# Delta rule: the values' convolution moved from VectorE to GpSimd, in a two-block kernel on one Trainium2 core

## What is computed

```python
def causal_depthwise_conv_2(x, w):        # width 4, one weight per channel and tap
    return lax.conv_general_dilated(x, w[:, None, :], window_strides=(1,),
        padding=[(CONV_WIDTH - 1, 0)], dimension_numbers=("NWC", "WIO", "NWC"), feature_group_count=c)

qkv_b = jax.nn.silu(causal_depthwise_conv_2(qkv_b, conv_w[i]))
q_b, k_b, v_b = jnp.split(qkv_b, 3, axis=-1)
qb = l2_norm(to_heads(q_b, N_HEADS_GDN))
kb = l2_norm(to_heads(k_b, N_HEADS_GDN))
vb = to_heads(v_b, N_HEADS_GDN)
...
o_b = gated_delta_rule(qb, kb, vb, g, beta)     # in chunks of 64 in the reference
```

## Time and profile before

| | us |
|---|---|
| median of 3 runs | 914.2 |
| lowest and highest | 913.17, 914.21 |
| the profiled execution: its own time | 914.48 |
| its span, from the first to the last instruction | 912.7 |
| PE busy in that span | 883.4 (97%) |
| DVE busy | 595.2 (65%) |
| ACT busy | 519.0 (57%) |
| POOL busy | 24.5 (3%) |

### The profile page before, as it was taken

How to read it: one execution, slowest core, us unless ns; L and a number is a source line. 1 busy time by engine, 2 the same in 40 slices (tenths; PEclk the granted TensorE clock), 3 DMA queues, 4 the chain that set the end, 5 groups by cost and what they waited for, 6 DMA issues and landing times. The chain is left out here.

```text
span 912.7 us, 17954 instructions
## 1 busy us (share of the span) xinstructions
PE 883.4 (97%) x7098; PEld 817.2 (90%) x7098; DVE 595.2 (65%) x971; ACT 519.0 (57%) x910; POOL 24.5 (3%) x36
## 2 busy tenths in 40 slices
PE   8999999999999999998989989899999999999998
PEld 6988899999998999998988979899988999999986
DVE  4689755555556666678685868666758554554576
ACT  6478754444446755657557374845459444444463
POOL 4100300000000000000000000000000000000000
PEclk8999999999999999999999999999999999999999
DMA  9813765555553454544223141415555555556541
GB/s 283 270 51 135 165 199 192 191 192 193 189 184 125 153 180 144 184 140 137 93 71 116 48 139 48 139 49 185 186 196 187 183 186 190 178 193 198 176 168 46
DMA packets 107655, 143.31 MB, mean 157 GB/s; under 512 B 3016, under 2 KB 95432, under 8 KB 107600
## 3 DMA queue, kind: packets, MB, share of 16 engines
q1 hardware_dynamic: 105648, 137.60, 46.6%
q0 software_dynamic: 1744, 4.74, 2.4%
q10 hardware_dynamic: 208, 0.20, 0.1%
HBM read 141.47 MB, written 1.05 MB: 156 GB/s over the span
## 5 line engine op out<-in xcount | busy, mean ns | idle before, releaser
L1180 DVE TENSOR_TENSOR wl<-w_raw,wh 128x1024 fp32r<-128x1024 f32 x251 | 305.3, 1224 | 228.3 <-ACT wh L634 227.7
L1794 PE MATMUL ps<-xTh,wh 128*128 128x256 f32 (+1 forms) x1160 | 331.9, 286 | 0.9 <-DVE xTl L1206 0.8
L1795 PE MATMUL ps<-xTl,wh 128*128 128x256 f32 (+1 forms) x1160 | 326.3, 281 | 0.0
L1796 PE MATMUL ps<-xTh,wl 128*128 128x256 f32 (+1 forms) x1160 | 326.3, 281 | 0.0
L634 ACT ACTIVATE wh<-w_raw 128x1024 fp32r<-128x1024 f32 x251 | 263.3, 1054 | 84.3 <-PE ps L1802 63.1
L1794 PEld LDWEIGHTS ps<-xTh,wh 128*128 128x128 f32 x1160 | 219.4, 189 | 5.0 <-issue 3.3
L1795 PEld LDWEIGHTS ps<-xTl,wh 128*128 128x128 f32 x1160 | 218.3, 188 | 2.1 <-issue 1.2
L1796 PEld LDWEIGHTS ps<-xTh,wl 128*128 128x128 f32 x1160 | 219.3, 189 | 0.0
L1800 PE MATMUL ps<-wh,y 128*128 128x512 f32 x224 | 87.9, 392 | 0.0
L1802 PE MATMUL ps<-wh,y 128*128 128x512 f32 x224 | 87.6, 391 | 0.0
L1801 PE MATMUL ps<-wl,y 128*128 128x512 f32 x224 | 87.1, 389 | 0.0
(11 more groups left out here) (380 smaller groups left out, 1274.1 us busy)
## 6 DMA issues: line engine op xcount, KB each, us to landing
w_raw<-in_w_in_dram SPq DMA_DIRECT2D x42, 1024.0 KB, 5.2
w_raw<-in_w_ff_dram SPq DMA_DIRECT2D x32, 1024.0 KB, 5.3
w_raw<-in_w_ffn_gate_dram SPq DMA_DIRECT2D x11, 1024.0 KB, 5.2
w_raw<-in_w_ffn_up_dram SPq DMA_DIRECT2D x11, 1024.0 KB, 5.3
w_raw<-in_w_ffn_down_dram SPq DMA_DIRECT2D x11, 1024.0 KB, 4.9
w_raw<-in_w_out_dram SPq DMA_DIRECT2D x8, 1024.0 KB, 5.0
w_raw<-in_w_proj_a_dram SPq DMA_DIRECT2D x4, 1024.0 KB, 5.1
w_raw<-in_w_proj_b_dram SPq DMA_DIRECT2D x4, 1024.0 KB, 5.2
```

Of the source, the lines that this page charges most:

```text
L1180: TT(low_part, raw_unit(SLOT[p], j, layout), high_part.bitcast(F32), ALU.subtract).then_inc(w_lo, 1)
L1794: mm(out, wh_, xh, start=first, stop=False)
L1795: mm(out, wh_, xl, start=False, stop=False)
L1796: return mm(out, wl_, xh, start=False, stop=last)
```

## The change

The values' convolution leaves DVE's list (stage 4 of the last attention round, stage 21 of the first three rounds of the delta rule) and becomes a loop of its own on GpSimd, four times. GpSimd waits until unit 5 of the pair has been copied out of PSUM, and from the second pair on until ACT has read the values of the pair before. It then scales by tap 0 into `cvn`, and for each further tap scales into a new buffer `vtap` (two scalings), waits for itself, adds `vtap` to `cvn` (two additions), and waits for itself again before the next tap. It reads the weights in `cw_all` directly. ACT waits on GpSimd's semaphore `cv_val` where it waited on DVE's `cv_out`, and `cv_out` counts two steps a pair instead of three. To make room for the semaphores, four of the first block are merged into others (each wait is for the same event as before). The new buffer takes 512 elements per partition, by which the region `R` grows from 16128 to 16578.

```diff
-REGION = 16128
+REGION = 16578
@@
+        vtap = carve(c4, 2, S)
@@ GpSimd
+            def value_conv(fu, stride, a, b):
+
+                for n in range(2):
+                    pool.wait_ge(emptied[n], along(AFTER[n], fu + 5, stride, a))
+                if b:
+                    pool.wait_ge(silu_v, b)
+                taps = cw_all.rearrange("p t (k h) -> p t k h", k=3)[:, :, 2, :]
+                for j in range(2):
+                    ins = pool.tensor_scalar(cvn[:, 4 + j, :], raw[:, 4 + j, 0:S], taps[:, 0, 2 * b + j:2 * b + j + 1], None, ALU.mult)
+                for tap in range(1, 4):
+                    for j in range(2):
+                        ins = pool.tensor_scalar(vtap[:, j, :], raw[:, 4 + j, tap:tap + S], taps[:, tap, 2 * b + j:2 * b + j + 1], None, ALU.mult)
+                    ins.then_inc(cv_tap, 1)
+                    pool.wait_ge(cv_tap, 5 * b + 2 * tap - 1)
+                    for j in range(2):
+                        ins = pool.tensor_tensor(cvn[:, 4 + j, :], cvn[:, 4 + j, :], vtap[:, j, :], ALU.add)
+                    if tap < 3:
+                        ins.then_inc(cv_tap, 1)
+                        pool.wait_ge(cv_tap, 5 * b + 2 * tap)
+                ins.then_inc(cv_val, 1)
+
+            pool.wait_ge(small2, 16 * 8)
+            pool.wait_ge(filled, 7)
+            value_conv(2 * P_MOBA + 32, 8, 0, 0)
+            for b in range(1, PAIRS):
+                value_conv(2 * P_GDN + 8, 8, b - 1, b)
+
             pool.wait_ge(mg_lo, 4)
@@ ScalarE, gdn_unit
-                        act.wait_ge(cv_out, (pair - 1) * 3 + (c // 2 + 1))
+                        if c < 4:
+                            act.wait_ge(cv_out, (pair - 1) * 2 + (c // 2 + 1))
+                        else:
+                            act.wait_ge(cv_val, pair)
@@ ScalarE, silu_keys and silu_values
-                act.wait_ge(cv_out, b * 3 + 2)
+                act.wait_ge(cv_out, b * 2 + 2)
...
-                act.wait_ge(cv_out, b * 3 + 3)
+                act.wait_ge(cv_val, b + 1)
@@ VectorE, moba_stage, stage 4
-                    if isinstance(a, int) and a == PAIRS - 1:
-                        conv_pair(2, 2 * P_MOBA + 32, 8, 0, 0)
@@ VectorE, conv_pair
-                    dve.wait_ge(silu_v if q == 2 else silu_qk, b)
+                    dve.wait_ge(silu_qk, b)
@@ VectorE, gdn_stage
-                if s == 21 and not final:
-                    conv_pair(2, 2 * P_GDN + 8, 8, a, a + 1)
@@ first block, merged semaphores (the pattern of all four)
-            act.wait_ge(sp_ready, 1)
+            act.wait_ge(vec_out, 2)
```

More of the change, by code:

```diff
@@ L377, in build @@
         small3 = sem("block_diag_loaded")
-        win_loaded, vec_ps, vec_out = sem("window_masks_loaded"), sem("vectors_in_psum"), sem("vectors_ready")
+        win_loaded, vec_ps, vec_out = sem("window_masks_loaded"), sem("vectors_in_psum"), sem("vectors_and_softplus_ready")
         gain_loaded = [sem("gain0_loaded"), sem("gain1_loaded")]
@@ L392, in build @@
         v1_out = sem("v1_ready")
-        lam_e, sp_ready, xc_ready = sem("lam_exp_ready"), sem("softplus_ready"), sem("conv_ready")
+        lam_e, xc_ready = sem("lam_exp_ready"), sem("conv_ready")
         scores_read = sem("attn1_scores_read")
@@ L396, in build @@
             sem(n) for n in ("lru_gates_in_psum", "lru_a_and_tanh_ready",
-                             "lru_mult2_ready", "lru_mult_ready"))
-        rec_out, rec_hi, rec_lo = sem("rec_ready"), sem("rec_hi_ready"), sem("rec_lo_ready")
+                             "lru_mult2_ready", "lru_mult_then_gelu_then_rec_hi_ready"))
+        rec_out, rec_lo = sem("rec_ready"), sem("rec_lo_ready")
         s1_ps, s1_max, s1_exp, p1T_ps, p1T_out, o1T_ps, o1T_hi, o1T_lo = (
@@ L401, in build @@
         i_act, p_ready = sem("lru_input_gate_ready"), sem("attn1_p_ready")
-        s1_sink, gelu_out = sem("attn1_sink_exp"), sem("gelu_ready")
+        s1_sink = sem("attn1_sink_exp")
         hid_s, hid_hi, hid_lo = (sem(n) for n in ("hid_square", "hid_hi", "hid_lo"))
@@ L420, in build @@
         xt_full = sem("inv_xt_blocks_copied")
+        cv_val, cv_tap = sem("gdn_value_conv"), sem("gdn_value_conv_tap")
         vb_out, sz_out, os_out = sem("gdn_vb_ready"), sem("gdn_gate_ready"), sem("gdn_o_copied")
@@ L805, in _ @@
                 act.wait_ge(emptied[b], EMPTIED[14][b])
-            act.activation(gy, gy, ACT.Gelu_apprx_tanh).then_inc(gelu_out, 1)
+            act.activation(gy, gy, ACT.Gelu_apprx_tanh).then_inc(mult_out, 1)
             for n in range(18, 20):
@@ L809, in _ @@
             act.wait_ge(rec_out, 1)
-            act.activation(yTh[:, 4:8, :], gy, ACT.Copy).then_inc(rec_hi, 1)
+            act.activation(yTh[:, 4:8, :], gy, ACT.Copy).then_inc(mult_out, 1)
             for n in range(20, 24):
@@ L1295, in _ @@
             TS(lam_t[:, 6, :], lam_t[:, 4, :], 8.0, None, ALU.mult)
-            TS(lam_t[:, 7, :], lam_t[:, 4, :], -8.0, None, ALU.mult).then_inc(sp_ready, 1)
+            TS(lam_t[:, 7, :], lam_t[:, 4, :], -8.0, None, ALU.mult).then_inc(vec_out, 1)
             for n in range(7, 10):
@@ L1379, in _ @@
             lo(17)
-            dve.wait_ge(gelu_out, 1)
+            dve.wait_ge(mult_out, 2)
             TT(gy, gy, r_g[:, :, META:T1], ALU.mult).then_inc(rec_out, 1)
             lo(18)
-            dve.wait_ge(rec_hi, 1)
+            dve.wait_ge(mult_out, 3)
             TT(yTl[:, 4:8, :], gy, yTh[:, 4:8, :].bitcast(F32), ALU.subtract).then_inc(rec_lo, 1)
@@ L1669, in _ @@
             pair_round(GDN_WEAVE, gdn_stage, pair_unit, G + 8, 0, 1)
-            for i in rounds(dve, 2, ch, 13):
+            for i in rounds(dve, 2, ch, 10):
                 pair_round(GDN_WEAVE, gdn_stage, pair_unit, G + 8, i + 1, i + 2)
```

## The result

The changed kernel takes 943.9 us (median of 4 runs, 942.5 to 945.1), the kernel before 913.7 us (median of 4, 911.3 to 914.2): a ratio of 1.033, with a 95% interval of 1.031 to 1.035. That is 30 us slower. Forecast were 923.6 us, 10 us slower, and a range up to 933. The direction was right, the size was a third.

A forecast was written before the change was run, and what follows sets the result against it. PE's list and few waits bound the kernel. GpSimd's 12.5 us a pair would make PE wait 7.8 + 2.4 + 0.9 = 11.1 us, giving 925.3 us from the 914.2 median; less 1.7 us of overlap, 923.6 us, range 915.5 to 933.0.

The forecast's parts named there:

- What bounds the kernel; DVE's relief is worth nothing: Whole kernel: PE's list, busy 97%, plus its few waits set the time; DVE's 13.3 us less work gains nothing.
- Where a late result is paid: Each round's start: late values delay ACT's SiLU, then DVE, then PE at L2155, with about 0.3 us of air.
- The threshold of 8.3 us: Pairs 1 to 3: the time from the raw values being ready until ACT asks for the convolved ones.
- The time on GpSimd: Values' convolution: 10.3 us of instructions, 1.0 of self-waits, 1.2 of slowing by DVE; 12.5 us a pair.
- the overlap taken off: GpSimd's back-to-back instructions: 0.07 us saved at eight places, 0.56 us a pair, 1.7 us over three pairs.
- the company of DVE: GpSimd beside DVE's three low parts: slowed by nothing up to 3.5 us; a third, 1.2 us, was taken.
- my third rival: GpSimd's chain: DVE's two-input instructions stop it in full, 14.8 us a pair, 934 us in all; chance 0.12.
- PE's waits: PE in front of L2155: 0.9 us for pair 0, 2.4 for pair 1, 3.9 each for pairs 2 and 3.
- The air in front of L2155: Between DVE's last multiplication and PE's product: 1.6 us in pair 0, 1.8 in pair 1, 0.3 in the others.
- the fifth rival: PE's clock at rounds' starts: added falls cost up to 7 us, or shifts remove two, 911 us; chance 0.03.
- the forecast's fourth rival: Pair 0: GpSimd stretches DVE's keys' convolution by 5.6 us, PE pays 3.8 us once, 927 us; chance 0.08.

The follow-up runs named there:

- two taps: Changed kernel with only taps 0 and 1 of the values' convolution on GpSimd, taps 2 and 3 left out of the computation: ratio 1.0004.
- moving the SiLU alone: Changed kernel with ScalarE's SiLU of the values moved from stage 0 to stage 3, behind the inverse norms: ratio 1.012 to the kernel before.
- without company: Changed kernel with GpSimd's convolution of pairs 1 to 3 started only after VectorE's last low part of the round: 956.0 us, ratio 1.045.
- the kernel before with the early SiLU: Kernel before, with ScalarE's SiLU and squares of queries and keys moved up from stage 0 to stage 21 (pairs 1 to 3): 905.5 us, ratio 0.990.
- the fill: Changed kernel with 20, 20, 28 and 28 products of zeros on TensorE in front of its new wait in stage 3: 937.8 us, ratio 1.027.
- the run with one addition: Changed kernel with one GpSimd addition of 128x512 per tap in place of two of 128x256: 940.7 us, ratio 1.028.
- the run with the work beside: Changed kernel with VectorE's convolution put back and read by ScalarE, GpSimd's same 56 instructions writing to unread scratch: ratio 1.0025 to the kernel before.
- the one with half the work: Changed kernel with GpSimd convolving only one of a pair's two value tiles and VectorE the other: ratio 1.0027 to the kernel before.

## Why the prediction was right in kind and wrong in size

- *What bounds the kernel; DVE's relief is worth nothing.* Right. No wait of PE went away with the 13.3 us of DVE's instructions except 0.9 us at the decays, and with two taps, where DVE has them all off its list and GpSimd is in time, the kernel took 1.0004 of the time before.
- *Where a late result is paid.* Right, and shown: the wait came at L2155's successor, in all four rounds, behind ACT's SiLU of the values, while the waits at the product with ones stayed. The threshold of 8.3 us held (two taps at 8.2 to 8.3 us: no loss), and moving the SiLU alone took 19 of the 30 us away.
- *The time on GpSimd.* This step failed in size: 12.5 us, or 11.9 with the overlap taken off, against 15.2 us. Two terms of the sum were too small. GpSimd's own work takes 12.0 us without company, against 10.7: a scaling in a row costs 0.92 us and not 0.79, an addition 0.71 and not 0.66, though a self-wait costs 0.09 and not 0.2 us. I had taken the fixed part from the memsets, 0.10 us; the row of 1024 elements and the new one of 256 give (2.35 - 0.73) / 768 = 2.1 ns an element and 0.19 us fixed for an addition, 2.5 ns and 0.28 us for a scaling. That the cost goes with the elements per partition, and not with the partitions, is consistent with these. The other term is the company of DVE, 1.2 us taken, 3.2 us measured: my third rival, at 0.12, came near it for GpSimd, and the "third" that I took had no row behind it. I had read the scaling of the earlier trace rows as perhaps stretched by the low part beside it. It was not. In the kernel before with the early SiLU such a low part lies inside that scaling whole, in the changed kernel none touches it (the first starts at 13.57), and it takes 2.85 us in both, as in the earlier trace rows. So this row on 16 partitions said nothing of what the company does to a scaling on 128; why that is so, no run shows. The rows of the one and of the other:

```profile
10.35 2.85 POOL L569 TENSOR_SCALAR R<-R,st 16x1024 f32<-16x1024 f32 x1 [1.74 <-DVE st L1275]
11.85 1.23 DVE L1180 TENSOR_TENSOR wl<-w_raw,wh 128x1024 fp32r<-128x1024 f32 x1
```

```profile
10.71 2.85 POOL L571 TENSOR_SCALAR R<-R,st 16x1024 f32<-16x1024 f32 x1 [1.48 <-DVE st L1307]
```

- *PE's waits.* 11.1 us forecast, 9.4 with the overlap off, 20.7 measured, in the order 4.4, 4.8, 6.5, 4.9 us instead of 0.9, 2.4, 3.9 and 3.9. Mostly this is the late chain: it took 15.1 to 15.4 us in the four rounds, against 12.5 us forecast and 13.5 us in the first. The air in front of L2155 was in part read wrong too. The 1.6 and 1.8 us of air in the first two rounds stood behind a fall of the clock, the 0.3 us in the others behind none. In the changed kernel the two short falls stand in the second and the fourth round, and there PE waits 4.8 and 4.9 us, against 6.5 us in the third. The first round had lost its air and waited more than the later chain alone explains, the fourth had gained some and waited less.
- *The clock.* Left out of the sum, and priced at up to 7 us in the fifth rival. It was 9.2 us by the remainder, 9.0 us by the work at half clock, and at least 6 by the fill. This is the second step that failed: the term stood at nothing in the sum. I treated as a chance what the profile of before had shown behind two of its four waits of 2.6 to 2.8 us; behind a wait of 4 us and more it came in every round.
- *GpSimd holds up DVE.* It did, but less than feared, and PE paid nothing for it: the six multiply-adds of the keys in the last attention round took 3.75 us, where they took 2.72 us before, and the forecast's fourth rival had 5.6 us for the eight instructions. ACT's SiLU of the keys starts at 426.93, no later than before (427.27).

The sum with the measured terms is 20.7 - 0.9 + 9.2 = 29.0 us. (The forecast of 923.6 us had 9.4 us there.) The two failed steps carry about equal parts of what was missing, 10 to 11 us of waits and 9 us of clock.

## What to carry to other kernels

Work moved to an idle engine is free only if its whole chain ends before the first reader asks; measure that window first (here 8.3 us), and hold the chain's highest price against it, company included, not the middle of a range. A result that is late on an engine which works through a fixed list holds up everything behind it in the list: TensorE did not need the values for another stage, but ScalarE stood in front of what it did need. And a wait of TensorE costs more than its length when the clock falls behind it; products of zeros in the wait gave back 6 us here, and moving one block of ScalarE's work into a gap of the kernel before gave 9 us, where relieving VectorE of the whole convolution gave nothing.

## What the runs showed of the hardware

Where VectorE's subtraction with two inputs in SBUF (128x1024, 1.22 us alone) and an instruction of GpSimd on 128 partitions overlap, one of them loses time. The Trainium skill ("SBUF — State Buffer", Who interferes with whom) has the one that starts second blocked until the first has finished. The traces agree in three cases. In the changed kernel GpSimd's scaling at 535.15 started second and lost 1.0 us under a low part that had 1.1 us to go, and its addition at 538.74 did the same. And VectorE starting second beside an addition is the one that loses: 0.35 us at 538.28, where the addition had 0.5 us to go, and 0.9 us at 537.16 in the run with one addition, where it had 1.0 us to go and kept its price of 1.27 us. They don't agree where VectorE starts second beside a scaling. In the last attention round its low part then took its usual time, and GpSimd, which had started first, lost 1.1 us:

```profile
426.31 2.93 POOL L610 TENSOR_SCALAR R<-R 128x256 f32<-128x256 f32 x2
426.41 1.21 DVE L1212 TENSOR_TENSOR wl<-w_raw,wh 128x1024 fp32r<-128x1024 f32 x1
```

Beside GpSimd's scaling on 16 partitions neither of them lost anything (2.85 and 1.23 us).

Without company, 128x256 elements cost GpSimd 0.92 us for a scaling by a value per partition, with one tensor as input, and 0.71 us for an addition of two: the instruction with one tensor is the dearer one. The same skill ("GPSIMD Engine Reference", section 4.1) expects instructions with one input to run at about line rate; the trace has 2.5 ns an element for them, more than the 2.1 ns of an addition, and VectorE's scaling of the same size takes 0.31 us.

PE's granted clock stood at 0.50 when PE went on behind each wait of 4.4 to 6.5 us, for 3.1 to 5.5 us of its work. With products of zeros in those waits it stood at 1.00 in all of them. Behind the waits of 2.6 and 2.8 us at the product with ones it fell in some rounds and not in others: in two of four in the kernel before, in three of four with the same waits in the run with the work beside and in the one with half the work.
